# Three key and query products of the next gated head on GpSimd instead of the vector engine, in a hybrid decoder layer

## What is computed

```python
def gla_chunked(q, k, v, log_a, s0, chunk):
    ...
    b = jnp.cumsum(gc, axis=2)
    b_last = b[:, :, -1:]
    q_dec = qc * jnp.exp(b)
    k_inv = kc * jnp.exp(-b)
    k_tail = kc * jnp.exp(b_last - b)
    a_intra = jnp.where(causal, jnp.einsum('nbihd,nbjhd->nbhij', q_dec, k_inv), 0.0)
    o_intra = jnp.einsum('nbhij,nbjhv->nbihv', a_intra, vc)

    def step(S, xs):
        qd, kt, vv, bl = xs
        o_inter = jnp.einsum('bihd,bhdv->bihv', qd, S)
        S = jnp.exp(bl[:, 0])[..., None] * S + jnp.einsum('bjhd,bjhv->bhdv', kt, vv)
        return S, o_inter
```

## Time and profile before

| | us |
|---|---|
| median of 3 executions | 1482.76 (1482.11 to 1484.5) |
| the profiled execution, device time | 1487.1 |
| span of its trace | 1485.2 |
| TensorE busy in it | 1369.7 (92%) |
| vector engine busy | 590.5 (40%) |
| GpSimd busy | 123.5 (8%) |
| head 0 of the last block | 1107.8 to 1136.5 |
| head 1 | 1136.5 to 1160.7 |
| head 2 | 1160.7 to 1183.5 |
| head 3, to the first branch product | 1183.5 to 1212.1 |

### The profile page before, as it was taken

How to read it: one execution, slowest core, us unless ns; L and a number is a source line. 1 busy time by engine, 2 the same in 40 slices (tenths; PEclk the granted TensorE clock), 3 DMA queues, 4 the chain that set the end, 5 groups by cost and what they waited for, 6 DMA issues and landing times. The chain is left out here.

```text
span 1485.2 us, 23583 instructions
## 1 busy us (share of the span) xinstructions
PE 1369.7 (92%) x9565; PEld 1194.3 (80%) x9565; DVE 590.5 (40%) x1253; ACT 632.6 (43%) x1078; POOL 123.5 (8%) x154
## 2 busy tenths in 40 slices
PE   4899999999989999999999999996569888899998
PEld 4899899998978888888888888885346667899876
DVE  4302113415624443444343323332668845454232
ACT  4212224412434557655675568553436631221111
POOL 2100001003201000000000000012200080000000
PEclk9899999999999999999999999998669989999999
DMA  7241453312222211122221121112533654544231
GB/s 203 78 142 35 116 106 94 108 48 63 62 54 53 58 53 53 52 58 58 59 59 55 57 59 59 44 54 81 219 119 127 221 184 132 165 129 115 83 109 70
DMA packets 140810, 137.19 MB, mean 92 GB/s; under 512 B 27040, under 2 KB 125680, under 8 KB 140512
## 3 DMA queue, kind: packets, MB, share of 16 engines
q1 hardware_dynamic: 137920, 127.27, 28.3%
q0 software_dynamic: 2784, 8.43, 1.9%
HBM read 97.82 MB, written 41.88 MB: 94 GB/s over the span
## 5 line engine op out<-in xcount | busy, mean ns | idle before, releaser
L217 PE MATMUL ps<-hH,wH 128*128 128x352 f32 (+1 forms) x1320 | 455.0, 345 | 9.0 <-DVE hL L502 6.9
L217 PE MATMUL ps<-hH,wL 128*128 128x352 f32 (+1 forms) x1320 | 428.2, 324 | 0.0
L217 PE MATMUL ps<-hL,wH 128*128 128x352 f32 (+1 forms) x1320 | 428.0, 324 | 0.0
L217 PEld LDWEIGHTS ps<-hH,wH 128*128 128x128 f32 (+1 forms) x1320 | 250.5, 190 | 59.9 <-issue 43.4
L217 PEld LDWEIGHTS ps<-hL,wH 128*128 128x128 f32 (+1 forms) x1320 | 251.4, 190 | 2.8 <-issue 1.9
L217 PEld LDWEIGHTS ps<-hH,wL 128*128 128x128 f32 (+1 forms) x1320 | 249.8, 189 | 0.9
L204 DVE TENSOR_TENSOR wL<-w_raw,wH 128x1024 fp32r<-128x1024 f32 (+1 forms) x55 | 66.8, 1214 | 191.4 <-ACT wH L196 191.4
L319 ACT ACTIVATE stg<-ps 128x352 f32<-128x352 f32 x132 | 61.2, 464 | 164.6 <-PE ps L217 157.7
L1219 DVE CUSTOM_DVE_ANT_0 sP<-ps,dist 128x128 f32<-128x128 f32 (+3 forms) x128 | 57.6, 487 | 108.7 <-PE ps L1057 72.0
L1270 ACT ACTIVATE pPT<-ps 128x512 f32<-128x512 f32 (+3 forms) x104 | 48.7, 468 | 110.0 <-PE ps L1057 109.9
L1311 ACT ACTIVATE sP<-sP,stat 128x640 f32<-128x640 f32 (+7 forms) x128 | 93.1, 729 | 2.6 <-DVE stat L1219 1.9
(11 more groups left out here) (336 smaller groups left out, 1993.1 us busy)
## 6 DMA issues: line engine op xcount, KB each, us to landing
w_raw<-in_w_in SPq DMA_DIRECT2D x46, 512.0 KB, 4.1
p_spill<-stg SPq DMA_DIRECT2D x132, 176.0 KB, 1.9
zt<-p_spill SPq DMA_DIRECT2D x24, 528.0 KB, 4.7
gvT<-p_spill SPq DMA_DIRECT2D x8, 528.0 KB, 6.3
rq<-p_spill SPq DMA_DIRECT2D x8, 528.0 KB, 6.9
x_all<-in_x_prompt SPq DMA_DIRECT2D x8, 512.0 KB, 10.1
w_raw<-in_w_in SPq DMA_DIRECT2D x16, 256.0 KB, 3.8
S<-in_state_gla SPq DMA_DIRECT2D x4, 1024.0 KB, 5.5
```

The source lines that it names most:

```text
L217: mm = nc.tensor.matmul(ps[0:t.m, bank, 0:NF], w[:, c % 2, t.m * k:t.m * k + t.m], x[:, k, NF * n:NF * n + NF], start=(k == 0 and i == 0), ...
```

## The change

For the heads 1 to 3 the three products `ki` (inverse-decayed keys), `W4` (weighted key tails) and `qi` (decayed inputs) are made by GpSimd. Head 0's stay on the vector engine, in the block before. A new function `on_pool` holds them; it is called for h = 1, 2, 3 ahead of GpSimd's other work in the block. GpSimd waits for ScalarE's exponentials and for `kt_ready` (the vector engine has made `kt`) before `ki`, and for `spans_ready` (the vector engine has made `dec`) before `W4`; `qi` follows without a wait. TensorE and ScalarE get a wait on `raw_read`, since `elem_done` of the vector engine no longer implies that `ki` is made. The arithmetic is the same.

```diff
@@ keys
             link(tt(kt[h % 2][:, :], rq[:, 1, :], ls[:, :], ALU.mult))
+            if h >= 1:
+                dve.sem_inc(sem("kt_ready"), 1)
@@ spans
             link(tt(d[:, :, 1:5], one[:, :, 0:1].to_broadcast([P, PT, 4]), d[:, :, 5:9], ALU.mult))
+            if h >= 1:
+                dve.sem_inc(sem("spans_ready"), 1)
-        def scaled(dst, src, h, c0, d0, n):
+        def scaled(dst, src, h, c0, d0, n, tt=tt):
+        def on_pool(pool, h):
+            i = h % 2
+            mul = nc.gpsimd.tensor_tensor
+            pool.wait_ge(sem("from_act"), 3 * h + 3)
+            pool.wait_ge(sem("kt_ready"), h)
+            mul(ki[i][:, :], rq[:, 1, :], e1[:, :], ALU.mult).then_inc(sem("raw_read"), 1)
+            pool.wait_ge(sem("spans_ready"), h)
+            scaled(W4[i][:, :, :].rearrange("p t (c i) -> p t c i", c=4), kt[i], h, 0, 12, 4, mul)\
+                .then_inc(sem("tails_ready"), 1)
+            scaled(by_chunk(qi[i]), qd[i], h, 0, 0, 4, mul).then_inc(sem("qi_ready"), 1)
@@ exps, ScalarE
                 act.wait_ge(sem("elem_done"), h)
+                act.wait_ge(sem("raw_read"), h)
@@ core, TensorE
                     pe.wait_ge(sem("elem_done"), h + 1)
+                    pe.wait_ge(sem("raw_read"), h + 1)
@@ GpSimd's queue in the last block
                 for s in cleared:
                     pool.sem_clear(s)
+                for h in range(1, GH):
+                    on_pool(pool, h)
@@ the vector engine's loop over heads
                     state(h, 1)
-                    if next1:
-                        inverses(dve, h + 1)
                     state(h, 2)
...
                     if next2:
                         tails(dve, link, h + 2)
-                    if next1:
-                        tail_sums(h + 1)
-                        inputs(h + 1)
```

## The result

| | before | after |
|---|---|---|
| first comparison: median of 18 executions each | 1482.62 (1478.79 to 1488.47) | 1495.4 (1483.32 to 1503.23) |
| the profiled execution, device time | 1487.1 | 1501.35 |
| its span, mean granted clock | 1485.2, 0.957 | 1499.6, 0.951 |

The changed kernel is slower: ratio 1.0083, 95% interval 1.0066 to 1.0101. The sign was forecast; the size, 1490.3 with a range to 1494.0, was not. Two later comparisons of the same two kernels gave 1.0066 (1.0035 to 1.0096) and 1.0062 (1.0036 to 1.0088). The medians of the first comparison lie 12.8 us apart. The mean of the kernel before in the four later comparisons and in `before_again` is 1485.0 (118 executions, one of 6383.55 us left out), and that of the changed kernel over its three comparisons 1494.9 (41): **9.9 us**. With the 18 executions of before from the first comparison it would be 10.1.

A forecast was written before the change was run, and what follows sets the result against it. TensorE, busy 92% of the span, bounds the kernel, so its waits for the vector engine matter. Heads 0, 1, 2 and the clock: 1.0 + 3.6 + 0.5 + 2.45 = 7.55 us on 1482.76, giving 1490.3; range 1484.5 to 1494.

The forecast's parts named there:

- The stalls: Vector products beside GpSimd's wait for its whole instruction less 0.14 us: `minus_abs` about 3.2, `Q0` near 2.5, `Q1` near 2.3.
- the 2.35 us bound: Upper bound for `W4` and `qi` on GpSimd if the repeated input saved nothing; 1.93 us was taken.
- The rival in which the vector engine gets both turns: `Q1` follows `Q0` before `qi` gets in, update 4 is 1.6 us earlier: 1486.5 to 1488.9; chance 0.10.
- the one without exclusion: In heads 0 to 2 `minus_abs`, `Q0` and `Q1` keep their 1.25, 0.95 and 0.69 us: 1482.6; chance 0.06.
- The chain: Delays reaching TensorE through late state updates in heads 0 to 2, without the clock: 5.1 us.
- Head 0: Late update 5 delays tile 6's L2024; late update 7 hides behind head 3's gates: +1.0 us.
- Head 1: Update 7 is late and moves TensorE's L2043 by 3.75 us, less at most 0.15 returned: +3.6 us.
- Head 2: No `minus_abs` here; update 4 is 2.8 us late and delays tile 5's L2024: +0.5 us.
- TensorE's wait before tile 6 of head 1: TensorE stands before tile 6's L2024, which reads the late update 5, for at least 1.2 us.
- the one before L2043: In head 1 TensorE waits for update 7 before the sample products, from 1158.0 to 1159.95.
- The clock: Waits at the end of head 1 drop TensorE's clock; L2043 to L1998 takes 10.5 for 8.05 us: +2.45.
- stalls larger than this, or further low clock stretches: Outcome beyond the forecast's own range, 1493 to 1497 us, mostly left out of the overall range; chance 0.10.

The follow-up runs named there:

- before_again: The kernel before, unchanged, run once more with a profile of its own: 1485.34 us, ratio 0.9995.
- before_fill: The kernel before with two extra matmuls each in heads 0 and 1 where TensorE waits for `ATs`: 1482.53 us, ratio 0.9988.
- fill_both: The changed kernel with four extra matmuls before L2043 of head 1 and two each at heads 0 and 1's `ATs` waits: 1491.28 us; repeated, 1490.96.
- beside_read: The kernel before, all vector work kept, plus three GpSimd products of the same shapes and places into an unread buffer: 1496.41 us, ratio 1.007.
- after_third: The changed kernel, unchanged, run another time beside the filled kernels: 1493.24 us, ratio 1.0062 against the kernel before.
- fill: The changed kernel with four extra matmuls in head 1 where TensorE waits before L2043: 1496.68 us (7 executions), ratio 1.0076 against the kernel before.
- fill_again: The kernel `fill` (four extra matmuls in head 1) run again unchanged: 1493.96 us, ratio 1.0062 against the kernel before.
- ki_only: The kernel before with only `ki` moved to GpSimd; `W4` and `qi` stay on the vector engine: 1490.4 us, ratio 1.002.
- wq_late: The kernel before with `W4` and `qi` on GpSimd, started only behind `sample`, beside the eight L2206; `ki` stays: 1486.35 us, ratio 1.0012.

## Why the prediction was right in its sign and missed in its size

The starts of L1998 and L2043 in heads 0 to 2 cut the heads into five parts. Their lengths in the profiled executions (us; L1998 and L2043 stand for the same lines of the other kernels too):

| part | before, again, third | before_fill | after, again, third | fill_both, again |
|---|---|---|---|---|
| head 0, L1998 to L2043 | 17.6, 17.6, 17.7 | 17.6 | 18.8, 18.8, 18.8 | 18.8, 18.8 |
| its sample part, L2043 to L1998 | 10.5, 10.5, 8.1 | 8.1 | 11.8, 10.5, 10.5 | 8.1, 8.1 |
| head 1, L1998 to L2043 | 15.7, 15.7, 15.7 | 15.7 | 18.7, 19.6, 19.7 | 19.8, 19.8 |
| its sample part | 8.1, 8.1, 8.1 | 8.1 | 11.9, 10.5, 10.5 | 8.1, 8.0 |
| head 2, L1998 to L2043 | 14.5, 14.5, 14.5 | 14.5 | 14.6, 14.5, 14.5 | 15.1, 15.1 |
| sum | 66.4, 66.4, 64.0 | 64.0 | 75.7, 73.9, 73.9 | 69.8, 69.8 |

The mean of before's three is 65.6, of after's three 74.5: 8.9 of the 9.9 us lie here. The remaining 1.0 is within the spread of the means (95%: about 1.7). Three traces stand for each kernel, so the low clock's part in this is a rough one.

**The stalls: right.** `minus_abs` 3.21 and 3.26 us (forecast about 3.2), `Q0` 2.22 (near 2.5), `Q1` 2.29 (near 2.3), `ki` 2.43 (2.42), `W4` 1.91 (1.93), `qi` longer by its wait. The Trainium skill's rule in "SBUF — State Buffer", section "Who interferes with whom", is borne out in each of them. The measured `W4` also settles the price against the 2.35 us bound, and against the 2.6 cycles an element of the Trainium skill's "GPSIMD Engine Reference", section "Elementwise — side-by-side cycle accounting", which only `ki` (2.43 us for 1056 columns) follows. The rival in which the vector engine gets both turns falls (`qi` went in between `Q0` and `Q1`), and the one without exclusion falls with `after` and `beside_read`.

**The chain: right.** From head start to head start the profiled execution took 30.5, 30.5 and 23.9 us (forecast 29.7, 30.2, 23.3). Without the clock, head 0 was forecast at +1.0 and is +1.1. Head 1 was forecast at +3.6 and has a mean of +3.6 in the changed kernel, +4.1 at the full clock. Head 2 was forecast at +0.5; it is 0.0 in the changed kernel and +0.56 where the clock stays up. The likely reason, read from the table, is that TensorE there reaches head 2 earlier and finds the vector engine late, while after a low clock it is late itself. TensorE's wait before tile 6 of head 1 (forecast at least 1.2 us) was split between tiles 5 and 6 (0.81 and 0.56 us in `after_third`), and the one before L2043 was 1.69 (forecast 1.95). The sum of these three at the full clock is 5.8 us, and by the times of `fill_both`, whose clock is that of before, 1490.8 (23 executions) less 1485.0 is 5.8 as well; with an interval of plus or minus 1.7, that the two agree so closely is luck. Forecast: 5.1.

**The clock: the step that failed.** The term of the sum that was mis-sized is the 2.45 us for TensorE's low clock, all of it at the end of head 1; the parts measure 4.1. Two things were wrong in it.
- The size at the end of head 1: the sample part took 11.9, 10.5 and 10.5, against 8.06; a mean of +2.9. I had taken the 10.5 of the earlier trace rows as what a low clock costs there. It is one of two prices.
- Head 0. I took its low clock for a constant, since it stands in the one trace of before, so that the change could add nothing. But it comes and goes in before (two of three executions) and was there in all three of the changed kernel, once 11.8 us long: means of 9.7 and 10.9, +1.2. Of this, 0.8 is the one execution of before without it and 0.4 the one long stretch, so it hangs on single executions.

Together +4.1 for 2.45. The mean granted clock of all executions says the same: 0.9606 for before (118), 0.9559 for the changed kernel (41), 0.961 for `fill_both` and its repeat (23). (Two executions, of `fill_both` and `before_fill`, whose recorded clock of 0.91 and 0.93 doesn't fit their times, are left out of the means of their kernels; with the first, `fill_both` and its repeat have 1491.1 us and 0.9591.) A clock lower by 0.0047 is 2 x 0.0047 x 1486 = 14.0 us more at 1.2 GHz. Among the 118 executions of before each such us goes with 0.39 us of time (0.44 among the 41 of the changed kernel). By 0.39, 5.5 us of the 9.9 are clock and 4.4 are left for the chain, where the cut by parts gives 4.1 for the clock and 4.8 for the chain (1.12 + 3.62 + 0.02). The two splits don't agree to a microsecond, but both make the clock about half of the loss.

**The rest of the 5.1 us.** 1495.4 lies 5.1 us above 1490.3, and the mis-sized clock is only part of that. The base of 1482.76 isn't: the kernel before had a median of 1482.62 in the same comparison, so the miss is in the difference, 12.8 us for 7.55, which is 5.2 too much (the base itself was 0.1 lower). Of this 1.4 are the sum of the parts (8.9 - 7.55: 1.65 too little for the clock, 0.3 too much for the chain as the changed kernel ran), 1.0 are outside the parts, and 2.9 are what the medians of this comparison show above the 9.9 of all executions (by rounding 0.1 too much in all). The later comparisons gave smaller ratios with overlapping intervals, so the 2.9 may be chance; no run explains them. The outcome had a line of its own in the prediction, "stalls larger than this, or further low clock stretches", 1493 to 1497 with a chance of 0.10, and the range to 1494 left most of it out. Its second half is what came.

What stays open: why the clock falls in one execution and not in the next of the same kernel behind the same waits (`fill` and `fill_again`); how large the gain of the filled waits is, since beside each other `fill_both` lay only 2.6 us under `after_third`, plus or minus 3.4, and the 4.1 (plus or minus 2.2) are means over several comparisons; and `ki_only`, whose profiled block was 103.5 us long while its mean lies 3.5 above before's; its mean clock, 0.9577, points to low stretches that this one execution didn't have, but no trace shows them.

## What to carry to other kernels

Before work goes to an idle GpSimd, look at what the vector engine runs in those microseconds: beside products out of two SBUF tiles the work is only added up; beside PSUM readers nothing stood in `wq_late`, though a later `qi` cost that kernel time by another path. Price the new waits of TensorE twice, in the chain and in its clock, and look at several executions before a low clock is called a constant: here it was about as costly as the stalls. And widen the range by the spread of the executions: three of them gave a base of 1482.76 that fitted the first comparison and lies 2.3 us under the mean of 118.

## What the runs showed of the hardware

- Between a vector instruction with two SBUF inputs and a GpSimd product the turn alternates, in each of three heads: `qi`, issued back to back with `W4`, stood until the waiting `Q0` had read (2.62 for 1.91 us), and `Q1` then stood for `qi`.
- Memsets of GpSimd (0.98 us for 1056 columns) kept nobody out: `minus_abs`, `Q0` and `Q1` took 1.25, 0.95 and 0.69 us beside them.
- A vector instruction that reads SBUF and PSUM didn't stand (L2219, 3.22 us for eight, with `qi` beside it in `wq_late`), but a small copy from SBUF to SBUF did beside `ki` (0.77 and 0.90 us for 0.18).
- A GpSimd product with one input repeated is cheaper than one with two full inputs: 1.91 us for 1024 columns, 2.43 for 1056.
- Filling TensorE's waits at the ends of heads 0 and 1 with some 2.7 us of idle matmuls brought back 4.1 us of the mean time (1494.9 to 1490.8, plus or minus 2.2), though the parts at full clock got no shorter. At the end of head 1 alone, 1.3 us of them did nothing that could be measured.
